# The experts' loops of a two-block network: sharing loop bounds, forming addresses before the waits, a branch hint on TensorE

## The reference

```python
def moe_ffn(h, w_rg, b_rg, w_re, b_re, w_gate, w_up, w_down):
...
    gate = g_w * jax.nn.softmax(top_v, axis=-1)      # two experts of 32 per token
    expert = g_idx[:, None] * EXPERTS_PER_GROUP + top_i.astype(jnp.int32)
...
    def expert_block(args):
        xblk, e = args
        hid = jax.nn.silu(xblk @ w_gate[e]) * (xblk @ w_up[e])
        return hid @ w_down[e]
```

## Time and profile before

| what | value |
|---|---|
| time, median of 3 (lowest to highest) | 4520.54 us (4517.87 to 4525.59) |
| the profiled execution's own time | 4520.74 us |
| its span in the profile | 4519.0 us |
| granted TensorE clock, mean | 0.959 |
| busy: TensorE, VectorE, ScalarE, GpSimd | 3849.0, 1608.9, 905.4, 271.6 us (85%, 36%, 20%, 6%) |

### The profile page before, as it was taken

One profiled execution on the slowest core, in us unless ns is written; L12 is line 12 of the kernel. 1 busy time (PEld: TensorE's weight loads), 2 busy tenths in 40 slices (PEclk: granted clock), 3 DMA queues, 4 the chain that ended last, 5 costly groups with the idle time before them and its releaser, 6 DMA issues.

```text
span 4519.0 us, 113553 instructions
## 1 busy us (share of the span) xinstructions
PE 3849.0 (85%) x45324; PEld 2478.6 (55%) x45325; DVE 1608.9 (36%) x3673; ACT 905.4 (20%) x2284; POOL 271.6 (6%) x453
## 2 busy tenths in 40 slices
PE   6997888999998899999897777777699987877774
PEld 3564665554445554446644666666444446766664
DVE  2676666223106641524634222222411142222214
ACT  3013444111003321311522111111200021111111
POOL 0000000000000000000001111111100002111111
PEclk9998999999999999999998999999799998999997
DMA  8101223002100001102413778885300225778784
GB/s 318 38 19 57 94 96 120 22 24 68 39 37 1 1 10 47 45 30 94 164 44 139 297 319 326 347 337 217 112 37 37 76 97 234 296 288 364 322 348 141
DMA packets 94346, 644.30 MB, mean 143 GB/s; under 512 B 18640, under 2 KB 41240, under 8 KB 60752
## 3 DMA queue, kind: packets, MB, share of 16 engines
q10 hardware_dynamic: 28896, 386.28, 20.5%
q1 hardware_dynamic: 46928, 194.98, 11.6%
q0 software_dynamic: 18336, 60.44, 4.1%
HBM read 594.70 MB, written 46.92 MB: 142 GB/s over the span
## 4 chain that ended last, share of the span: by engine, by line
PE 48%; issue 5%; DVE 4%; DVEq 2%; DMA 2%; ACT 1%; POOLq 0%; POOL 0%; SPq 0%; ACTq 0%
PE banks L258 22%; PE banks L2387 14%; PE banks L2396 7%; DVEq L2290 1%; DMA arena<-y_tok,arena 1%; PE banks L2382 1%; PE banks L1519 1%; PE banks L2378 1%; DVE arena L2525 1%; DVE arena L1634 1%; PE banks L2118 1%; DVEq L2525 1%; DMA h_tok<-arena 0%; PE banks L467 0%; PE banks L1568 0%
## 5 line engine op out<-in xcount | busy, mean ns | idle before, releaser
L258 PE MATMUL banks<-arena 128*128 128x512 f32 (+2 forms) x4544 | 1749.4, 546 | 38.8 <-ACTq L137 16.9
L258 PEld LDWEIGHTS banks<-arena 128*128 128x128 f32 x4544 | 840.3, 191 | 935.9 <-issue 885.0
L2387 PE MATMUL banks<-arena 128*32 128x128 f32 x20480 | 658.7, 280 | 138.2 <-issue 130.2
L2387 PEld LDWEIGHTS banks<-arena 128*32 128x32 f32 x20480 | 571.9, 112 | 208.4 <-issue 206.7
L2396 PE MATMUL banks<-arena 128*32 128x128 f32 x10240 | 341.7, 290 | 168.6 <-DVE arena L2525 168.3
L2396 PEld LDWEIGHTS banks<-arena 128*32 128x32 f32 x10240 | 301.8, 117 | 207.5 <-issue 206.4
L2490 DVE COPY arena<-banks 128x128 f32 x162 | 47.2, 291 | 491.4 <-PE banks L2382 488.2
L1588 PE MATMUL banks<-arena 128*64 128x128 f32 x1952 | 161.7, 284 | 55.1 <-ACT arena L1601 39.4
L945 DVE SCALAR_TENSOR_TENSOR arena<-arena 128x1024 f32<-128x1024 f32 x240 | 195.9, 878 | 0.2 <-DVEq L137 0.2
L2353 POOL DMA_INDIRECT arena<-h_tok,arena x176 | 171.9, 977 | 142.2 <-POOL arena L2350 136.5
L301 DVE SCALAR_TENSOR_TENSOR arena<-banks,arena 128x512 f32<-128x512 f32 (+1 forms) x72 | 51.9, 721 | 333.2 <-PE banks L258 333.2
(11 more groups left out here) (327 smaller groups left out, 3257.6 us busy)
## 6 DMA issues: line engine op xcount, KB each, us to landing
arena<-in_w_gu ACTq DMA_DIRECT2D x120, 2048.0 KB, 7.4
arena<-in_w_dn ACTq DMA_DIRECT2D x60, 2048.0 KB
arena<-in_w_ada SPq DMA_DIRECT2D x24, 2048.0 KB, 7.3
y_tok<-arena SPq DMA_DIRECT2D x648, 32.0 KB
arena<-in_w_gu SPq DMA_DIRECT2D x8, 2048.0 KB, 9.2
y_tok<-arena POOLq DMA_DIRECT2D x1, 12800.0 KB, 36.0
arena<-in_ab_w_ada SPq DMA_DIRECT2D x6, 2048.0 KB, 9.7
arena<-in_cd_w_ada SPq DMA_DIRECT2D x6, 2048.0 KB, 7.2
```

The lines of the kernel that those rows point to most:

```text
L258: last = pe.matmul(self.bank_of(g, n), lhsT, rhs, start=k == 0, stop=k == KT - 1)
L2387: last = pe.matmul(bank(2 + part)[32 * q:32 * q + 32, 0:128], xbT[:, 128 * j + 32 * q2:128 * j + 32 * q2 + 32], w_gu[slot][part][:, 2 * q2 ...
```

## The change

Three things change in the experts' stages.

1. `in_turn` now loads the bounds itself and hands them to the closures as `begin` and `end`. A value loaded for one loop is used again for the others that need it: the outer loop has four loads a turn in place of eight. Two stand at the head of a turn, one between the first gate_up and the first down, one between that down and the second gate_up, none ahead of the second down. The tail starts with two loads and makes one more per pair. The last bounds are returned, so that the code behind `in_turn` loads nothing.
2. Ring addresses are formed by `snap` into a register ahead of the waits, on VectorE (`keep_hid`, L2514, down) and on ScalarE (down).
The matmuls, copies, transfers and semaphores stay as they are.

```diff
@@ -2304,16 +2304,26 @@
 
             def in_turn(self, eng, first, second):
 
-                first(0, 0)
+                c0, c1 = self.cum(eng, 0), self.cum(eng, 1)
+                first(0, 0, c0, c1)
                 with eng.Fori(0, E // 2 - 2) as p:
-                    first(2 * p + 1, 1, p)
-                    second(2 * p, 0, p)
-                    first(2 * p + 2, 0, p + 1)
-                    second(2 * p + 1, 1, p)
+                    c1, c2 = self.cum(eng, 2 * p + 1), self.cum(eng, 2 * p + 2)
+                    first(2 * p + 1, 1, c1, c2, p)
+                    c0 = self.cum(eng, 2 * p)
+                    second(2 * p, 0, c0, c1, p)
+                    c3 = self.cum(eng, 2 * p + 3)
+                    first(2 * p + 2, 0, c2, c3, p + 1)
+                    second(2 * p + 1, 1, c1, c2, p)
+                c0, c1 = self.cum(eng, E - 4), self.cum(eng, E - 3)
                 for i in range(E - 3, E):
-                    first(i, i % 2)
-                    second(i - 1, (i - 1) % 2)
-                return
+                    c2 = self.cum(eng, i + 1)
+                    first(i, i % 2, c1, c2)
+                    second(i - 1, (i - 1) % 2, c0, c1)
+                    c0, c1 = c1, c2
+                return c0, c1
+
+            def trips(self, eng, begin, end):
+                return nc.Fori(begin, end, engines=bass.OrderedEngineSet([eng.engine]), hint_back_edge=True)
 
             def blocks_sp(self, sp):
                 sp.wait_ge(stage_end, closed(("ev_attn", "od_conv")[self.l]))
@@ -2406,14 +2416,13 @@
                 pe.wait_ge(self.xr[0], 1)
                 self.turn_x(pe).then_inc(self.xt[0], 1)
 
-                def gate_up(i, slot, nth=None):
+                def gate_up(i, slot, begin, end, nth=None):
                     nth = i // 2 if nth is None else nth
-                    begin, end = self.cum(pe, i), self.cum(pe, i + 1)
                     pe.wait_ge(self.wa[slot], 16 * nth + 16)
                     pe.sem_inc(passed, 1)
                     pe.wait_ge(self.wb[slot], 16 * nth + 16)
                     pe.sem_inc(passed, 1)
-                    with pe.Fori(begin, end) as b1:
+                    with self.trips(pe, begin, end) as b1:
                         pe.wait_ge(self.x0, b1)
                         pe.wait_ge(self.ma, b1)
                         self.gu_half(pe, slot, 0, 0)
@@ -2426,12 +2435,11 @@
                         self.gu_half(pe, slot, 1, 0).then_inc(self.gb0, 1)
                         self.gu_half(pe, slot, 1, 1).then_inc(self.gb, 1)
 
-                def down(i, slot, nth=None):
+                def down(i, slot, begin, end, nth=None):
                     nth = i // 2 if nth is None else nth
-                    begin, end = self.cum(pe, i), self.cum(pe, i + 1)
                     pe.wait_ge(self.wd[slot], 16 * nth + 16)
                     pe.sem_inc(passed, 1)
-                    with pe.Fori(begin, end) as b1:
+                    with self.trips(pe, begin, end) as b1:
                         pe.wait_ge(self.y0, b1)
                         pe.wait_ge(self.h0, b1)
                         self.dn_half(pe, slot, 0, (0, 1))
@@ -2441,19 +2449,19 @@
                         self.dn_half(pe, slot, 1, (0, 1)).then_inc(self.dm, 1)
                         self.dn_half(pe, slot, 1, (2, 3)).then_inc(self.d1, 1)
 
-                self.in_turn(pe, gate_up, down)
-                pe.wait_ge(self.mb, self.cum(pe, E))
+                begin, top = self.in_turn(pe, gate_up, down)
+                pe.wait_ge(self.mb, top)
                 pe.sem_inc(passed, 1)
                 self.turn_hid(pe)
-                down(E - 1, 1)
+                down(E - 1, 1, begin, top)
 
             def blocks_act(self, a):
                 a.sem_inc(self.sb, 1)
                 a.sem_inc(self.y0, 1)
                 a.sem_inc(self.y1, 1)
 
-                def gate_up(i, slot, nth=None):
-                    with a.Fori(self.cum(a, i), self.cum(a, i + 1)) as b1:
+                def gate_up(i, slot, begin, end, nth=None):
+                    with a.Fori(begin, end) as b1:
                         a.wait_ge(self.ga, b1)
                         a.activation(sg[:, 0:64], bank(2)[:, 0:64], ACT.Silu).then_inc(self.sa, 1)
                         a.wait_ge(self.gb, b1)
@@ -2463,9 +2471,9 @@
                         for part in range(2):
                             self.load_gu(a, slot, e, part)
 
-                def down(i, slot, nth=None):
-                    with a.Fori(self.cum(a, i), self.cum(a, i + 1)) as b1:
-                        room = (b1 & (XB - 1)) * 256
+                def down(i, slot, begin, end, nth=None):
+                    with a.Fori(begin, end) as b1:
+                        room = a.snap((b1 & (XB - 1)) * 256)
                         a.wait_ge(self.yf, b1)
                         a.sem_inc(passed, 1)
                         a.wait_ge(self.d0, b1)
@@ -2475,9 +2483,8 @@
                     if nth is not None or i + 2 < E:
                         self.load_dn(a, slot, self.expert(a, i + 2))
 
-                self.in_turn(a, gate_up, down)
-                down(E - 1, 1)
-                top = self.cum(a, E)
+                begin, top = self.in_turn(a, gate_up, down)
+                down(E - 1, 1, begin, top)
                 for half in (self.y0, self.y1):
                     a.wait_ge(half, top)
                     a.sem_inc(half, 1)
@@ -2486,8 +2493,9 @@
                 return d.tensor_copy(xbT[:, P * j:P * j + P], bank(0)[:, P * j:P * j + P])
 
             def keep_hid(self, d, b1):
+                at = d.snap((b1 & (HELD - 1)) * 128)
                 d.wait_ge(self.ht, b1)
-                d.tensor_copy(held[:, bass.ds((b1 & (HELD - 1)) * 128, 128)], bank(4)[:, 0:P]).then_inc(self.he, 1)
+                d.tensor_copy(held[:, bass.ds(at, 128)], bank(4)[:, 0:P]).then_inc(self.he, 1)
 
             def blocks_dve(self, d):
                 d.sem_inc(self.yf, 6)
@@ -2502,39 +2510,39 @@
                 d.wait_ge(self.x_ok[1], 1)
                 d.tensor_copy(xr, xb[:, 256:512]).then_inc(self.xr[1], 1)
 
-                def gate_up(i, slot, nth=None):
-                    with d.Fori(self.cum(d, i), self.cum(d, i + 1)) as b1:
+                def gate_up(i, slot, begin, end, nth=None):
+                    with d.Fori(begin, end) as b1:
                         d.wait_ge(self.sb, b1)
                         d.tensor_tensor(hid[:, 64:128], sg[:, 64:128], bank(3)[:, 64:128], ALU.mult).then_inc(self.mb, 1)
                         self.keep_hid(d, b1)
                         d.wait_ge(self.sa, b1)
                         d.tensor_tensor(hid[:, 0:64], sg[:, 0:64], bank(2)[:, 64:128], ALU.mult).then_inc(self.ma, 1)
+                        at = d.snap(((b1 + 1) & (XB - 1)) * 256)
                         d.wait_ge(self.x_ok[2], b1)
                         d.wait_ge(self.xt[1], b1)
-                        d.tensor_copy(xr, xb[:, bass.ds(((b1 + 1) & (XB - 1)) * 256, 256)]).then_inc(self.xr[1], 1)
+                        d.tensor_copy(xr, xb[:, bass.ds(at, 256)]).then_inc(self.xr[1], 1)
                         d.wait_ge(self.he, b1)
                         d.wait_ge(self.gb0, b1)
                         self.turned_half(d, 0).then_inc(self.x0, 1)
                         d.wait_ge(self.gb, b1)
                         self.turned_half(d, 1).then_inc(self.x1, 1)
 
-                def down(i, slot, nth=None):
-                    with d.Fori(self.cum(d, i), self.cum(d, i + 1)) as b1:
-                        at = ((b1 + 1) & (HELD - 1)) * 128
+                def down(i, slot, begin, end, nth=None):
+                    with d.Fori(begin, end) as b1:
+                        at = d.snap(((b1 + 1) & (HELD - 1)) * 128)
                         d.wait_ge(self.dm, b1)
                         d.tensor_copy(hidS[:, 0:64], held[:, bass.ds(at, 64)]).then_inc(self.h0, 1)
                         d.wait_ge(self.d1, b1)
                         d.tensor_copy(hidS[:, 64:128], held[:, bass.ds(at + 64, 64)]).then_inc(self.h1, 1)
 
-                self.in_turn(d, gate_up, down)
-                top = self.cum(d, E)
+                begin, top = self.in_turn(d, gate_up, down)
                 d.wait_ge(self.sb, top)
                 d.sem_inc(passed, 1)
                 d.tensor_tensor(hid[:, 64:128], sg[:, 64:128], bank(3)[:, 64:128], ALU.mult).then_inc(self.mb, 1)
                 self.keep_hid(d, top)
                 d.wait_ge(self.he, top)
                 d.sem_inc(passed, 1)
-                down(E - 1, 1)
+                down(E - 1, 1, begin, top)
 
             def sum_pool(self, g):
                 for i in range(KT):
```

## The result

The changed kernel took 4481.45 us (median of 4, 4479.25 to 4486.57), the kernel before beside it 4523.07: a ratio of 0.991, 95% interval 0.9893 to 0.9927, a gain of 41.6 us between the medians. It is faster, as forecast, but the forecast of 4445 with its range of 4404 to 4480 is missed by 36 us, and the range by 1.5. The profiled execution has a span of 4477.5 us (before: 4519.0) and a mean granted clock of 0.96.

What follows compares the result with a forecast made beforehand. TensorE was taken to set the end, idling in the expert stages before down and gate_up. Loads -71.0, addresses -14.4, hint +14.4 and clock -5 gave -76 from 4520.7, so 4445 us, range 4404 to 4480.

Steps and rivals of the forecast that it cites:

- Loads ahead of down: Passages from gate_up into down lose one or two value loads: gains of 17.4, 31.6 and 2.5 us.
- Loads ahead of gate_up: 28 passages from down into gate_up lose one TensorE load of 0.65 us: 18.2 us, plus 1.3 in the tails.
- Addresses ahead of waits: Between down blocks, VectorE's two register steps move ahead of the wait, 0.15 us each of 96 times: 14.4 us gained.
- The hint: One more instruction per trip of TensorE's loops, 0.09 us on 160 gate_up trips: 14.4 us lost, bounds -6 and +29.
- The clock: Less time at TensorE's lower granted clock as the longest idle stretches shrink: -5 us, between -25 and +10.
- The hint that undoes residency: At TensorE's loop heads the hint undoes what is resident, so the kernel gets slower, from 0.40 us per taken edge; chance 0.08.
- The hint that removes the pause: Gate_up's pauses are fetches behind taken branches; the hint removes them, 52 us more gained, 4393 us; chance 0.06.
- Another wait in place of the loads: ScalarE's queue or the pause holds down back in 34 passages, and VectorE's address step stays: 4480 us; chance 0.09.

Runs made afterwards that it cites:

- experiment 14: Kernel without hint, bounds carried in registers, but TensorE's two loads a turn ahead of gate_up, not down: 4300.19 us, ratio 0.9596 to the kernel before.
- experiment 3: Changed kernel without the hint, ring addresses moved by reg_mov into an allocated register ahead of the waits: 4428.27 us, ratio 0.9796 to the kernel before.
- experiments 1: Changed kernel with only the hint taken out of TensorE's loops: 4440.41 us, ratio 0.9821 to the kernel before.
- 2: Kernel before with only the hint added to TensorE's loops: 4563.37 us, ratio 1.0095 to the kernel before.
- 9: Changed kernel, word for word, run again on another slow chip: 4479.41 us, ratio 0.99 to the kernel before.
- 10: Changed kernel without the hint, run again on that second slow chip: 4436.4 us, ratio 0.9797 to the kernel before.
- 16: Changed kernel, word for word, run again on a third slow chip: 4482.52 us, ratio 0.993 to the kernel before.
- 17: Changed kernel without the hint, run again on the third slow chip: 4435.76 us, ratio 0.9827 to the kernel before.
- experiment 8: Kernel before, word for word, run again on the second slow chip: 4523.78 us.
- 15: Kernel before, word for word, run again on the third slow chip: 4517.43 us.
- experiment 4: Kernel before without POOL's gathers in the second layer after its first eight blocks: 4485.67 us, one run.
- experiment 5: Changed kernel with the hint only in TensorE's loops inside the outer loop: 4403.22 us on a quick chip, ratio 0.982 to the kernel before.
- 18: Changed kernel without the hint, bounds carried in registers, VectorE's down address early, on the third slow chip: 4313.02 us, ratio 0.9557 to the kernel before.

## Why the prediction was wrong

**Loads ahead of down: right.** Forecast 17.4 + 31.6 + 2.5 = 51.5 us; from before to the kernel without the hint the 62 waits into down fell from 144.0 to 89.5, so 54.5. The working behind one part was right only by its number. I had down start at T + 1.25, held by the pause that the gather brings TensorE; it starts at T + 1.14, and what holds it is VectorE's copy, 0.41 us long while the gather runs. On the quick chips, without the pause, the passage has the same 1.2 us. ScalarE stayed hidden, as worked out: in the passage without a load its transfers are issued by 2654.16 and its copy of down's first half starts at 2654.86.

**Loads ahead of gate_up: right within 5 us.** 18.2 + 1.3 forecast; the 60 waits there fell by some 15 us without the hint. The price of a load on TensorE, 0.65, holds for the second of two loads: in the median such a passage lost 0.64. The last load of a passage costs more, 0.77 (experiment 14).

**Addresses ahead of waits: 14.4 forecast, nothing measured.** The step that failed is "two register steps, 0.15 us, of which `snap` takes both ahead of the wait"; the section on the change says the same of `snap` and is wrong in it. The lower bound, nothing, was the truth, though not for the reason given there. The price of the steps was right: experiment 3 gets 0.15 us a block for them (14.7 us over 98), as forecast.

**The hint: +14.4 forecast, +41 to +47 measured.** This is the step that failed most, and it made most of the miss: "I take 0.09" for each of 160 trips, where what was measured lies above even the bound of +29. Its steady part was sized well where it counts: 0.12 us per passage into gate_up (0.09 taken), nothing in down, as forecast. At gate_up's back-edges, for which 8.6 us stood, little is left: the trip grows by 0.02 to 0.04 us. What the prediction did not have are the single stops, 27 to 31 us in eight or nine places, less 2 to 7 at the first layer's start: it priced the hint per trip, from the duration of neighbouring instructions, and looked for an instruction fetch only in the laps. By experiments 1, 2, 9 against 10 and 16 against 17, the hint is the cause, and the q8 packets show that the long stops are waits for instructions. The rest, which differs from profile to profile, is longer matmuls, in part at the lower clock. The taken branch, which the good end of the bound had at 0.076, got longer, here in the changed kernel and then without the hint:

```profile
L2425 PEldq COMPARE_BRANCH  x160: 71/223/238, 2479.7 to 4379.3; - x160
```

```profile
L2425 PEldq COMPARE_BRANCH  x160: 67/207/219, 2479.2 to 4345.9; - x160
```

**The clock: -5 forecast.** Without the hint the runs give 4520.23 - 4440.41 = 79.8 us, of which the loads' passages are 54.5 + 15 = 69.5. The 10 left are for the most part the clock: the time lost to it over all blocks fell from 59.2 to 46.8 us, by 12.4, from experiment 8 to 10 by 21.6 and from 15 to 17 by 10.1. So the sign and the bounds hold, and the size was half of what came or less. The way was as the prediction had it: the stretches before down got short, and 25 blocks of down at the lower clock became none. But the turns of 2.0 us stayed, and more of the blocks of gate_up behind them fell to it, 27 at a mean clock under 0.85 in place of 15. That took 19.7 us back. (The range, too, took only 11 us of clock on its low side, where the term's own bound left 20.)

So the sum without its failed terms, -71 - 5 = -76, met 80 (82 to 89 in the later lots), and errors of 14 and 27 us in one direction, less the 4 by which the rest did better, made the 36 us. That 4445 lies so near the 4440 of the kernel without the hint is luck: two wrong terms, -14.4 and +14.4, cancel in the sum.

**The rivals.** The hint that undoes residency: not so. In the laps of the changed kernel, 2512 to 3037 us, q8 moved one packet, as in the earlier trace rows; the stops lie in the first passes and in the tails. But its core, that a hint lets TensorE wait for instructions, was right, and my term had nothing for it. The hint that removes the pause: refuted by experiment 4, and by the changed kernel, which keeps it. The rule of the Trainium skill cited there ("Runtime: NRT & Kernel Launch", Instruction fetch mechanics), that a taken branch to a target outside the resident window forces a fetch, is not borne out or refuted for the laps, where q8 moved that one packet; no run here shows the hint bringing a gain by it. Another wait in place of the loads: its 4480 is what was measured, by other causes; the 34 passages kept their gain. Only its second half, that the address steps give nothing, came true.

## What to carry to other kernels

A branch hint is one more instruction on the queue, and here it cost far more than its 31 ns: try it alone, and look for it not only in the loop but in "issue" in the first and last passes, beside the packets of the instruction queue. A load into a register costs by its place: put it where its engine waits for another, and carry what the next turn needs in a register. Before counting a gain for an address formed early, see in the trace's rows of that line that its steps really left the wait. Idle time has a second price in the clock: a turn cut from 2.0 to 0.61 us also gave 1.6 us in most blocks behind it.

## What the runs showed of the hardware

- The 0.54 us pause of TensorE at the end of a software gather differs from chip to chip: it is there in the profiles of the three slow chips and in the first two, absent in all kernels profiled on the two quick ones.
- A copy from SBUF to SBUF on VectorE takes 0.41 us in place of 0.195 where it runs beside such a gather (the changed kernel's L2534: 195/195/417 ns). The Trainium skill ("VectorE: DVE Perf Modes", Two Vector instructions with no wait between them) says that some Vector operations read through a second interface to SBUF that is shared with GpSimd; that fits, and no run here tests it.
- With the hint TensorE stopped for 2.7 to 8.8 us around packets of the instruction queue and went on 1.3 to 2.0 us after each had landed, 21 times in three profiles; without it packets landed as often and it didn't (experiments 9 and 10).
- With the hint the like loop head took 0.1 us in one layer and 1.1 in the other, in every turn and with no such packet (experiment 5). Why isn't shown.
- Behind idle stretches of 2.0 us the granted clock of the next block was 0.71 in 19 of 28 outer turns; behind stretches of 0.61 us it was 1.00 (experiments 17 and 18).
